# Differential attention: the half swap of the rotary step by small transfers instead of permutation matmuls

## The reference, cut to what matters

```
half = ROT_DIM // 2                      # 8
r1 = tf[..., :half];  r2 = tf[..., half:ROT_DIM]
out = concatenate([r1 * c - r2 * s, r1 * s + r2 * c, tf[..., ROT_DIM:]])
s = einsum('bqhcd,bkhcd->bhcqk', q, k) * scale       # two components c, causal mask
a = softmax(s)[:, :, 0] - lam * softmax(s)[:, :, 1]
o = einsum('bhqk,bkhe->bqhe', a, v)
```

## Time and profile before

| | us |
|---|---|
| median of 3 runs | 3184.14 (3183.85 to 3186.23) |
| the profiled execution | 3186.78 |
| its span, first to last instruction | 3184.9 |
| span before the prologue | 0 to 2318 |
| prologue of the stage | 2318 to 2359.5 |
| loop over m = 0 to 27, with the rotary steps | 2359.5 to 2545.5 |
| rest of the stage | to about 2620 |

### The profile page before, as it was taken

One profiled execution on the slowest core, in us unless ns is written; L12 is line 12 of the kernel. 1 busy time (PEld: TensorE's weight loads), 2 busy tenths in 40 slices (PEclk: granted clock), 3 DMA queues, 4 the chain that ended last, 5 costly groups with the idle time before them and its releaser, 6 DMA issues.

```text
span 3184.9 us, 40021 instructions
## 1 busy us (share of the span) xinstructions
PE 3043.3 (96%) x13896; PEld 2378.4 (75%) x13896; DVE 1432.6 (45%) x2125; ACT 1281.1 (40%) x1950; POOL 1249.1 (39%) x565
## 2 busy tenths in 40 slices
PE   7999999999997899999999989999989999899998
PEld 4667888878775688888666778888867787788886
DVE  4444555235524425552398433332267762433323
ACT  4555444234444434442323534443333343344332
POOL 4213444444354244444423424444432254144443
PEclk8999999999997899999999999999999999999999
DMA  3112223333220133333222313223321233133332
GB/s 134 46 34 73 92 92 93 105 94 96 75 66 1 29 105 97 93 92 100 79 67 86 99 40 93 92 93 98 100 71 60 60 113 93 40 92 93 95 98 90
DMA packets 73903, 260.52 MB, mean 82 GB/s; under 512 B 8640, under 2 KB 8896, under 8 KB 73536
## 3 DMA queue, kind: packets, MB, share of 16 engines
q1 hardware_dynamic: 69552, 249.07, 25.7%
q10 hardware_dynamic: 3600, 7.36, 0.6%
q0 software_dynamic: 640, 2.62, 0.3%
HBM read 256.92 MB, written 2.10 MB: 81 GB/s over the span
## 4 chain that ended last, share of the span: by engine, by line
PE 66%; issue 20%; POOL 8%; DVE 4%; ACT 2%; ACTq 0%; POOLq 0%; DMA 0%; DVEq 0%; SPq 0%
PE bank L733 16%; PE bank L734 16%; PE bank L735 16%; POOL w_lo L626 8%; PE bank L1237 1%; PE bank L1185 1%; PE bank L1186 1%; PE bank L1187 1%; PE bank L849 1%; PE bank L950 1%; PE bank L850 1%; PE bank L851 1%; PE bank L1362 1%; DVE bank L1955 1%; DVE acc L2049 1%
## 5 line engine op out<-in xcount | busy, mean ns | idle before, releaser
L626 POOL TENSOR_TENSOR w_lo<-w_raw,w_hi 128x1024 fp32r<-128x1024 f32 (+1 forms) x465 | 1104.1, 2376 | 1673.7 <-ACT w_hi L2235 1673.5
L2235 ACT ACTIVATE w_hi<-w_raw 128x1024 fp32r<-128x1024 f32 (+1 forms) x483 | 503.2, 1043 | 716.3 <-DMA w_raw<-w_glu_out 157.3
L733 PE MATMUL bank<-xh,w_hi 128*128 128x512 f32 x1864 | 745.1, 400 | 4.4 <-DVE xl L1464 4.4
L734 PE MATMUL bank<-xl,w_hi 128*128 128x512 f32 x1864 | 739.7, 397 | 0.0
L735 PE MATMUL bank<-xh,w_lo 128*128 128x512 f32 x1864 | 739.6, 397 | 0.0
L733 PEld LDWEIGHTS bank<-xh,w_hi 128*128 128x128 f32 x1864 | 351.8, 189 | 93.2 <-DVE xl L1464 5.7
L734 PEld LDWEIGHTS bank<-xl,w_hi 128*128 128x128 f32 x1864 | 351.7, 189 | 87.5 <-issue 2.6
L735 PEld LDWEIGHTS bank<-xh,w_lo 128*128 128x128 f32 x1864 | 351.5, 189 | 85.8
L735 PE MATMUL bank<-hh,w_lo 128*128 128x512 f32 x704 | 279.1, 396 | 0.0
L733 PE MATMUL bank<-hh,w_hi 128*128 128x512 f32 x704 | 279.1, 396 | 0.0
L734 PE MATMUL bank<-hl,w_hi 128*128 128x512 f32 x704 | 279.1, 396 | 0.0
(11 more groups left out here) (345 smaller groups left out, 4567.3 us busy)
## 6 DMA issues: line engine op xcount, KB each, us to landing
w_raw<-w_ffn_in SPq DMA_DIRECT2D x88, 512.0 KB, 3.5
w_raw<-w_glu_in SPq DMA_DIRECT2D x88, 512.0 KB, 3.5
w_raw<-w_ffn_out SPq DMA_DIRECT2D x48, 512.0 KB, 3.5
w_raw<-w_glu_out SPq DMA_DIRECT2D x48, 512.0 KB, 3.6
w_raw<-w_ssm_in SPq DMA_DIRECT2D x41, 512.0 KB, 3.5
w_raw<-w_pw SPq DMA_DIRECT2D x24, 512.0 KB, 3.5
w_raw<-w_diff_in SPq DMA_DIRECT2D x24, 512.0 KB, 3.5
w_raw<-w_attn_in SPq DMA_DIRECT2D x18, 512.0 KB, 3.6
```

Source lines behind the costliest of these rows:

```text
L626: pool.tensor_tensor(w_lo[:, slot, 0:n], w_raw[:, slot, 0:n], w_hi[:, slot, 0:n].bitcast(F32), ALU.subtract).then_inc(w_split, 1)
L733: pe.matmul(b, wh, hi[:, k, 0:n], start=(k == 0), stop=False)
L734: pe.matmul(b, wh, lo[:, k, 0:n], start=False, stop=False)
L2235: act.activation(w_hi[:, slot, 0:n], w_raw[:, slot, 0:n], ACT.Copy).then_inc(w_half, 1)
```

## The change

The permutation tile `rot` and its load go, and with them the 16 matmuls of `turn_rope`. A tile `d_rot` of 128 by 512 (in memory that `m_v` uses later) is cleared once; for each rotary step ScalarE issues four transfers of 8 rows of 2 KB from the key or query tile into it, and line 1657 reads `d_rot` in place of the PSUM bank. The minus sign goes into the frequency column, and so into the sine table. Before its four transfers ScalarE waits for the eviction of the chunk and for the previous reading of `d_rot` (`r_t`).

```
# PE
-                pe.wait_ge(tab_done, 1)
-                turn_rope(0, 0)
-                feed(6)
-                turn_rope(0, 1)
-                feed(2)
+                feed(8)
...
-                    if i == 1 and s < KD:
-                        turn_rope(s, 0)
...
-                    if i == 2 and s < KD:
-                        turn_rope(s, 1)
# DVE
-                    dve.wait_ge(tab_in, 48)
+                    dve.wait_ge(tab_in, 32)
...
-                    dve.wait_ge(r_rot, n + 1)
+                    dve.wait_ge(r_rot, 64 * (n + 1))
...
-                    dve.tensor_tensor(c_rope, bank[6][:], sine[:], ALU.mult).then_inc(r_t, 1)
+                    dve.tensor_tensor(c_rope, d_rot, sine[:], ALU.mult).then_inc(r_t, 1)
...
+                dve.memset(d_rot, 0.0).then_inc(r_clear, 1)
                 mixing()
...
                 evict(0)
                 tables()
+                dve.wait_ge(tab_done, 1)
                 evict(1)
# ACT
-                act.dma_start(rot[:], A["rot"]).then_inc(tab_in, 16)
...
+                def swap_halves(h, query):
+
+                    n = 2 * h + query
+                    act.wait_ge(bank_free, BANKS + st.chunk0 + 3 * h + query + 1)
+                    if n:
+                        act.wait_ge(r_t, n)
+                    else:
+                        act.wait_ge(r_clear, 1)
+                    src = d_q[:, h, :] if query else d_k[:, h % RING, :]
+                    for lo in (0, 8, 64, 72):
+                        other = lo ^ 8
+                        act.dma_start(d_rot[lo:lo + 8, :], src[other:other + 8, :]).then_inc(r_rot, 16)
...
+                swap_halves(0, 0)
                 next_slab()
                 next_slab()
+                swap_halves(0, 1)
                 for m in range(DM + 2):
...
                     slabs_fed(m, 3)
+                    if i < 2 and h + 1 < KD:
+                        swap_halves(h + 1, i)
```

More of the change, by code:

```diff
@@ L251, in build @@
         sine = sb("sine", [P, S])
-        rot = sb("rot", [P, P])
+        d_rot = m_v[:, 0, 0:S]
         freq = sb("freq", [P, 1])
@@ L531, in build @@
         lam_in, lam_sum, lam_exp = sem("lam_in"), sem("lam_sum"), sem("lam_exp")
+        r_clear = sem("r_clear")
         o_dia, o_bc = sem("o_dia"), sem("o_bc")
@@ L1033, in feed @@
                         next(work, None)
[L1035 to L1044, removed]
                 def turn_value(h):
                     pe.wait_ge(bank_free, BANKS + st.chunk0 + 3 * h + 3)
-                    pe.wait_ge(r_t, 2 * h + 2)
+                    if h:
+                        pe.wait_ge(v_ready, 2 + v0 + h)
                     for t in range(NT):
@@ L2801, in interleave @@
     return np.ascontiguousarray(w.reshape(k, 2, half // P, P).transpose(0, 2, 1, 3)).reshape(k, 2 * half)
-EXTRA = {"ssm": ("cst",), "attn": ("cst", "rel_t", "sinks"), "conf": ("memt",), "diff": ("memt", "cst", "pos", "freq", "rot", "lam")}
+EXTRA = {"ssm": ("cst",), "attn": ("cst", "rel_t", "sinks"), "conf": ("memt",), "diff": ("memt", "cst", "pos", "freq", "lam")}
 def constants():
@@ L2823, in rotary @@
     freq = np.zeros((P, 1), np.float32)
-    rot = np.zeros((P, P), np.float32)
     for base in (0, 64):
         for i in range(8):
[L2827 to L2830, removed]
+            freq[base + 8 + i] = 500000.0 ** (-i / 8)
+            freq[base + i] = -freq[base + 8 + i]
+    return freq
 def attn_in_cols(w):
@@ L2868, in layout @@
                          I["diff_lambda_k2_2"][0]]).reshape(1, 256)
-    A["freq"], A["rot"] = rotary()
+    A["freq"] = rotary()
     A["w_pw1"] = pack(interleave(I["conv_w_pw1_2"][0], D))
```

## The result

The changed kernel took 3192.69 us (median of 14 runs, 3189.04 to 3196.85) beside 3184.82 us for the kernel before (14 runs): ratio 1.0022, interval 1.0014 to 1.0030. It is slower by about 7 us. The forecast was a gain of 4.4 us with a range of 3171 to 3190, so it had the wrong sign and the measured time lies outside the range.

The account below looks back on a forecast made before the run. PE was taken to bound the loop, with the VectorE and ScalarE chain next. A loop gain of 2.5 us plus 1.9 in the prologue made 4.4: 3184.1 - 4.4 = 3179.7 us, range 3171 to 3190.

Parts of the forecast that it names:

- PE's gain: In the loop, two permutation matmuls of 0.86 us go per period: 1.72 us a period, 12.0 us in all.
- The chain in the loop: VectorE and ScalarE work to a head's last exponentials ends at 25.00 of 27.18 us, 2.2 us of slack; loop gains 2.5.
- d: Delay the change adds to the VectorE and ScalarE chain per head: 1.25 + 0.25 = 1.5 us; loop gains 13.0 - 7 d.
- the price of an issue: ScalarE's four query transfers ahead of block 2's exponentials, 1.9 us plus 0.05 for the semaphore, make them 1.25 us later.
- a sign of being wrong: Issues much longer than the loads' would show the forecast wrong; d then grows by the excess, 7 us for each us.
- The key's rope: In each head it ends 0.25 us later, between nothing and 0.65, as VectorE's SBUF operands meet GpSimd's split.
- My bounds: Limits for four transfer issues on ScalarE: four of 0.34 us (1.4) and four of 0.65 us (2.6).
- rival (D): PE's waits ahead of heads lower its clock, 1.7 us a fall; 3191.6 with all seven, mostly over 3188; chance 0.18.
- the key's transfers: In ScalarE's block 0 they wait for an eviction 2.8 us before the next exponential; 1.9 us of issues fit in.
- The prologue: Ahead of the first score: earlier lambda load, issues, landings and caught splits, yet a gain of 1.9 us.
- The earlier load of lambda: In the prologue, one load less ahead of lambda's moves all to the eviction of chunk 0 earlier by 0.48 us.
- Landing: Swapped rows arrive 2.2 us after issue, hidden ahead of the rope in the loop; at 3.4 us it costs 0.35.

Follow-up runs that it names:

- e1: Changed kernel without its 64 transfers and the wait for them, the rotated part left out: 3173.95 us, ratio 0.9961 to the kernel before.
- e10: Changed kernel, swaps split between ScalarE and SyncE, prologue weight halves first, SyncE's first swap behind load 5, query evicted before the old output's copy: 3172.33 us, ratio 0.9963.
- e11: Changed kernel with its 64 transfers reading 8 rows of an input in HBM instead of key or query in SBUF: 3178.10 us, ratio 0.9974.
- e3: Changed kernel with its four issues copying sine-table rows into a tile nobody reads, the rope waiting for none: 3189.25 us, ratio 1.0010.
- e2: Changed kernel with two of the four transfers of each swap, rows 64 to 79 left out: ratio 0.9975 to the kernel before.
- e6: Changed kernel with each swap's transfers divided, rows 0 to 15 by ScalarE and 64 to 79 by SyncE: 3179.04 us, ratio 0.9979.
- e12: e10 with ScalarE issuing its half of head 0's key swap before its two weight halves in the prologue: 3177.01 us, ratio 0.9968.
- e7: e6 with ScalarE's two weight halves moved ahead of the first swap in the prologue: ratio 0.9997 to the kernel before.
- e8: Changed kernel with transfers of 16 rows instead of 8, without the exchange of halves: ratio 1.0026 to the kernel before.
- e5: Changed kernel with all four transfers of each swap issued by SyncE behind a weight load, none by ScalarE: 3181.72 us, ratio 0.9985.

## Why the prediction was wrong, by its steps

**PE's gain: right.** Periods at PE's limit were given as 25.46 and are 25.47 in e1 and e10.

**The chain in the loop: the mechanism right, the issue mis-sized.** PE waits for ScalarE's exponentials, as forecast, though only 0.4 us of it stands ahead of a head's first score and 1.1 to 1.4 ahead of block 3's, where the forecast had it all at the first. Per middle head d was taken at 1.5 and came out at 2.1 (27.14 less 25.00). The step that failed is the price of an issue: the nearest rows were four loads, taken at 0.47 each, 1.9 for four. They took 2.62, and the exponential stands 2.75 behind the eviction instead of 1.95: 0.80 too little. The prediction had named this as a sign of being wrong, at 7 us for each us of excess; the excess of 0.72 for the four gives 5.0. The key's rope was put at 0.25 and cost 0.07 in the heads with 27.14 (2.14 less 2.07) and about 0.3 in two others. The forecast gave the sum of the periods as 183.5 (24.48 and six of 26.50); it is 190.97, of which 3.6 lie in the middle heads, 0.6 in the last and 3.25 in head 0. e11 shows what the rows had in common and the transfers had not: their source was HBM. My bounds reached 2.6 for four, so the measured value lay at their very end; I chose the value by the nearest rows in place and queue, when kind of source was the nearness that counted.

**Head 0: the clock, and the key's issues.** Beyond the 25.1 that d = 2.14 gives, head 0 takes 2.6 us more. The granted clock after the 4.01 wait and after the one of 1.89 (columns as in the earlier trace rows):

```profile
2361.90:2365.30 3.40, 3.40 (x12) 2.71 (x12) 1.98 (x9) 1.79 (x5) 0.99 (x1) 0.51 0.00 0
2382.30:2385.70 3.40, 3.40 (x12) 2.72 (x11) 3.37 (x3) 0.00 (x0) 2.73 (x1) 0.50 0.01 2
```

This is rival (D), in one head of seven: two stretches at 1.2 GHz. It explains 1.65 us and not all 2.6: e3 has the same issues, no long wait in the prologue and no fall of the clock, and its head 0 takes 26.08. Most of the difference is there before block 1, 1.58 us after the first of the two stretches. The other 1.0 us stands without any fall. The prediction gave the key's transfers 2.8 us and said that 1.9 fit in. In head 0 there are only 2.2 (the key's eviction ends 4.7 us after the first score, block 1's exponential stands at 6.88 in the kernel before), and four issues of 2.61 do not fit. In e3, whose first score is at 2356.13, the exponential stands at 7.42:

```profile
2360.89 2.61 ACTq L2332 DMA_DIRECT2D m_v<-sine  x4
2363.55 0.47 ACT L2346 ACTIVATE a_prob_t<-bank,a_stat 128x256 f32<-128x256 f32 x1 [3.94 <-DVE a_stat L1651]
```

That is 0.54 of the 1.0, the same mis-sized term once more, and with two issues (e2, e6) it is gone. Most of the rest is in the two ropes, whose caught operations are longer than in the kernel before (2.89 against 2.53 for the query's).

The other heads' waits of 1.1 to 1.4 us were followed by no fall. Over the runs, the three waits of 3.6 us and more were each followed by one, those of up to 1.56 in heads 0 to 6 never, though one of 1.04 ahead of head 7 in e12 was, and between 1.6 and 2.1 it went either way (1.62 in e7, 1.89 here and 2.06 in e8 with; 1.62 in e6 and 1.90 in e3 without). A head with one fall in it took 1.6 us more in e7 (25.83 against 24.22 in e6) and 2.2 in e8 (29.13 against 26.97), near the 1.7 of the prediction. The measured time lies where the prediction expected (D), but the falls are a small part of the loss.

**The prologue: the wrong sign.** The forecast from the eviction was 12.9 us (14.32 less the gain of 1.9, of which 0.48 was lambda's and lies ahead of it); it is 15.95. Up to the splits the story was right, and the splits caught the first two operations of the key's rope. But the four issues took 3.24 us, not 1.9, and the query's transfers could only start when the first rope operation had ended (2353.4, forecast 2351.3). They took 2.99 to issue and were read at 2359.16; the forecast had them landed at 2355.0 and read at 2355.5:

```profile
2346.02 3.24 ACTq L2330 DMA_DIRECT2D m_v<-d_k  x4
...
2350.50 5.21 POOL L627 TENSOR_TENSOR w_lo<-w_raw,w_hi 128x1024 fp32r<-128x1024 f32 x2 [12.34 <-ACT w_hi L2220]
...
2350.61 2.83 DVE L1640 TENSOR_TENSOR acc<-m_v,sine 128x512 f32<-128x512 f32 x1 [2.84 <-DMA m_v<-d_k]
2353.36 2.88 DVE L1641 TENSOR_TENSOR d_k<-d_k,cosine 128x512 f32<-128x512 f32 x1
...
2353.53 2.99 ACTq L2330 DMA_DIRECT2D m_v<-d_q  x4
...
2359.16 0.69 DVE L1640 TENSOR_TENSOR acc<-m_v,sine 128x512 f32<-128x512 f32 x1 [1.59 <-DMA m_v<-d_q]
```

Here issues, landing and the operations that the splits catch follow one another in one chain, and an error in each adds up, 3.0 us. The earlier load of lambda brought about 0.1 us and not 0.48: VectorE's wait went from 1.67 to 0.88 beside 0.48 of clearing, but its product started only 0.14 us earlier counted from the first load's issue: the load was issued 0.49 us earlier, as forecast, and landed 3.59 us after its issue began instead of 3.24.

**Landing: nothing in the loop, as said** (e3, in sum), though longer than the 2.2 taken: from the start of the key's last issue (they end at 2423.89, less one of 0.66: 2423.2) to the rope at 2426.78 it is some 3.5 us. It would have begun to cost as soon as the issues moved away, as e5 shows.

**In sum** the misses are 7.5 us in the periods, 3.0 in the prologue and 0.3 for lambda: 10.8 of the 11.4 between the forecast's gain of 4.4 and the measured loss of 7.

What stays open: which part of an issue from SBUF takes the second 0.33 us, and why waits of nearly equal length are followed by a fall of the clock or not. Why the first issue of a burst in the prologue takes longer was not tried either.

## What to carry to other kernels

Count a DMA issue as work of the engine that issues it: put its duration on that engine's timeline, between the instructions it stands between, even if the page calls the engine idle. Take the price from rows with the same kind of source, and where no row has it, let the range's far end be as likely as the middle. Put many small transfers on queues with nothing urgent behind them (here all on SyncE gave 0.9985 and half on each 0.9979, too close to rank by time), and read each queue that gets a wait for what is queued behind that wait, as e7 showed. Before moving an operand of VectorE from PSUM to SBUF, look at what GpSimd runs beside it.

## What the runs showed of the hardware

- An issue of 8 rows of 2 KB took 0.63 to 0.66 us from SBUF to SBUF (0.61 with 16 rows) on ScalarE's queue and about as much on SyncE's, and 0.33 us from HBM to SBUF with the same shape. The Trainium skill (DMA: Bandwidth & Descriptors, "Rules for kernel authors") advises to join many small transfers into one large one. Here that would have helped through the issuing engine's time, for DMA's share of the loop stayed at 0.20.
- The first issue of a burst can take longer: four took 3.24 us in the prologue (the first 1.24) and 2.62 in the loop.
- From the last issue to the first use a 16 KB transfer within SBUF took about 3.5 us beside a weight load (DMA share about 0.7 from 2422 to 2424), and about 2.0 in a quiet stretch (0.09) in e5, whose issues end at 2420.34, so that the last began at 2419.7, and whose rope began at 2421.71.
